# Products of keys with themselves taken two heads at a time, in the thirds that also turn keys into tokens

## What is computed

```
gc = cumsum(g)
decay[i,j] = exp(gc[i] - gc[j])            for i >= j, else 0
lower[i,j] = beta[i] * (k[i] . k[j]) * decay[i,j]   for i > j, else 0
t_mat      = inverse(I + lower)
u = t_mat @ (beta * v);  w = t_mat @ (beta * k * exp(gc))
```

## Time and profile before

| | |
|---|---|
| median of 3 runs | 354.02 us (353.72 to 354.14) |
| the profiled execution | 354.62 us, span 352.8 us |
| TensorE busy (PE) | 345.2 us, 98% of the span |
| VectorE (DVE) | 269.7 us, 76% |
| ScalarE (ACT) | 220.5 us, 62% |
| GpSimd (POOL) | 61.0 us, 17% |
| TensorE's granted clock, mean | 0.998 of 2.4 GHz |

### The profile page before, as it was taken

One profiled execution on the slowest core, in us unless ns is written; L12 is line 12 of the kernel. 1 busy time (PEld: TensorE's weight loads), 2 busy tenths in 40 slices (PEclk: granted clock), 3 DMA queues, 4 the chain that ended last, 5 costly groups with the idle time before them and its releaser, 6 DMA issues.

```text
span 352.8 us, 7457 instructions
## 1 busy us (share of the span) xinstructions
PE 345.2 (98%) x2753; PEld 332.2 (94%) x2753; DVE 269.7 (76%) x565; ACT 220.5 (62%) x499; POOL 61.0 (17%) x112
## 2 busy tenths in 40 slices
PE   8999999999999999999999999999999999999993
PEld 6889998999999999999999999999999999999882
DVE  4869897499986868978789797887967557588644
ACT  4778895455466667686866867677667655444421
POOL 2535535500033000300203011030200201000011
PEclk9999999999999999999999999999999999999999
DMA  7958948996799564655555565655555556775703
GB/s 233 274 140 225 304 125 201 236 289 171 209 248 218 134 180 126 163 133 153 146 150 149 131 170 129 171 132 146 143 159 143 171 158 181 208 240 186 260 32 119
DMA packets 100321, 62.48 MB, mean 177 GB/s; under 512 B 4692, under 2 KB 95230, under 8 KB 100286
## 3 DMA queue, kind: packets, MB, share of 16 engines
q1 hardware_dynamic: 98030, 58.59, 60.6%
q0 software_dynamic: 1072, 3.04, 3.0%
q10 hardware_dynamic: 1184, 0.39, 0.5%
HBM read 60.41 MB, written 1.59 MB: 176 GB/s over the span
## 4 chain that ended last, share of the span: by engine, by line
PE 97%; DVE 1%; issue 1%; POOL 0%; ACT 0%; DVEq 0%; POOLq 0%; ACTq 0%
PE banks L1347 67%; PE banks L1365 6%; PE banks L1560 6%; PE banks L1256 2%; PE banks L1445 1%; PE banks L1422 1%; PE banks L1462 1%; PE banks L1451 1%; PE banks L1332 1%; PE banks L1291 1%; PE banks L1507 1%; PE banks L1479 1%; PE banks L1483 1%; PE banks L1512 1%; PE banks L1487 1%
## 5 line engine op out<-in xcount | busy, mean ns | idle before, releaser
L890 DVE TENSOR_TENSOR w_lo<-raw,w_hi 128x1024 fp32r<-128x1024 f32 x102 | 124.1, 1218 | 44.4 <-ACT w_hi L637 43.9
L637 ACT CAST w_hi<-raw 128x1024 fp32r<-128x1024 f32 x103 | 107.5, 1047 | 10.0 <-PE banks L1560 5.5
L1347 PE MATMUL banks<-h_hi,w_hi 128*128 128x256 f32 x568 | 81.4, 286 | 0.0
L1347 PE MATMUL banks<-h_hi,w_lo 128*128 128x256 f32 x568 | 76.6, 278 | 0.0
L1347 PE MATMUL banks<-h_lo,w_hi 128*128 128x256 f32 x568 | 76.6, 278 | 0.0
L1347 PEld LDWEIGHTS banks<-h_hi,w_hi 128*128 128x128 f32 x568 | 71.0, 189 | 0.3
L1347 PEld LDWEIGHTS banks<-h_hi,w_lo 128*128 128x128 f32 x568 | 69.9, 188 | 0.0
L1347 PEld LDWEIGHTS banks<-h_lo,w_hi 128*128 128x128 f32 x568 | 69.9, 188 | 0.0
L974 DVE SCALAR_TENSOR_TENSOR acc<-banks,vec,acc 128x255 f32<-128x255 f32 (+2 forms) x72 | 34.5, 479 | 4.0 <-ACT acc L761 2.1
L587 POOL TENSOR_TENSOR so<-so,rnq 128x2 f32<-128x2 f32 x8 | 2.6, 328 | 162.8 <-ACT junk L828 162.8
L761 ACT ACTIVATE acc<-banks,vec 128x256 f32<-128x256 f32 x16 | 7.6, 474 | 18.7 <-PE banks L1347 18.7
(11 more groups left out here) (243 smaller groups left out, 548.3 us busy)
## 6 DMA issues: line engine op xcount, KB each, us to landing
raw<-in_w_in_dram SPq DMA_DIRECT2D x79, 512.0 KB, 4.0
raw<-in_w_branch_dram SPq DMA_DIRECT2D x16, 512.0 KB, 3.7
raw<-in_w_out_dram SPq DMA_DIRECT2D x8, 512.0 KB, 3.3
xin<-in_x_dram SPq DMA_DIRECT2D x2, 512.0 KB, 3.9
th_E<-g_rows POOLq DMA_DIRECT2D x2, 512.0 KB, 6.6
bias<-bias_rows POOLq DMA_DIRECT2D x1, 1024.0 KB, 8.2
raw<-in_x_dram SPq DMA_DIRECT2D x2, 512.0 KB, 4.4
out_dram<-xin SPq DMA_DIRECT2D x4, 256.0 KB, 2.0
```

The costliest lines, as they stand in the source:

```text
L637: nc.scalar.copy(w_hi[:, t % SLOTS, :], raw[:, t % SLOTS, :]).then_inc(s_hi, 1)
L890: v.tensor_tensor(w_lo[:, t % SLOTS, cols], raw[:, t % SLOTS, cols], w_hi[:, t % SLOTS, cols].bitcast(F32), ALU.subtract).then_inc(s_lo, 1)
L1347: last = mm(ps, w, r, start=part == 0 and k == 0, stop=part == 2 and k == KT - 1)
```

## The change

Three tables of step numbers change, and the two loops that read `SIM` now take a tuple of heads.

- The products of a head with itself are issued for two heads in one third: heads 0 and 1 at S = 27, 2 and 3 at S = 32, 4 and 5 at S = 36, 6 and 7 at S = 42. VectorE's multiplications for these heads stand at the same step numbers.
- The turns of heads 6 and 7 go from S = 35 and 41 to 36 and 42. With that each of the four thirds that holds products also holds a turn, and ScalarE's squares for these heads stand at S = 37 and 43.
- `E0` goes from 26 to 24, so ScalarE's exponentials for head h stand at S = 24 + h.

```diff
-TOKENS = {10: 0, 16: 1, 19: 2, 24: 3, 27: 4, 32: 5, 35: 6, 41: 7}
-SIM = {28: 0, 29: 1, 30: 2, 31: 3, 36: 4, 37: 5, 42: 6, 43: 7}
-E0 = 26
+TOKENS = {10: 0, 16: 1, 19: 2, 24: 3, 27: 4, 32: 5, 36: 6, 42: 7}
+SIM = {27: (0, 1), 32: (2, 3), 36: (4, 5), 42: (6, 7)}
+E0 = 24
...
-                if S in SIM:
-                    similarity(SIM[S])
+                for j in SIM.get(S, ()):
+                    similarity(j)
```

## The result

The changed kernel takes 355.58 us (median of 20 executions), the kernel before 354.11 us (20 executions, 353.72 to 354.59). The ratio is 1.0029, with an interval of 1.002 to 1.0038: slower by 0.3%. I had forecast no change, 353.9 us within 353.1 to 354.9.

A forecast was written before the change was run, and what follows sets the result against it. TensorE, with 97% of the chain, was taken to bound the kernel. From the profiled 354.62 us, minus 0.17 for breaks plus 0.1 for a wait gave 354.55, so a median of about 353.9 us, range 353.1 to 354.9.

The forecast's parts named there:

- what bounds: Whole kernel: TensorE holds 97% of the chain and shows no wait after start-up; faster ScalarE or VectorE is worth nothing.
- the work: TensorE: the change adds and removes no instruction, with 32 key product records and 16 turn records; term 0.
- the breaks: TensorE, S = 27 to 43: eight of twelve breaks go, saving 0.17 us, with bounds 0 and 0.9 us.
- the new wait: TensorE's turn of head 5 at S = 32 waits for its keys, 0 to 0.15 us; taken as 0.1.
- the price of a break beside key thirds: TensorE: a key third between breaks takes 0.95 us, 0.04 over the plain 0.907; three such breaks go.
- The rival with drains: TensorE: every break drains the array, so eight breaks would give back 1.3 us, 352.7 us; chance 4%.
- Term: 0: Blocks' store, load and inversion, 0.7 to 0.8 us later: margin at 113.68 shrinks from 1.2 to 0.5 us and holds.
- the inversion starts at 70.7: VectorE's inversion after the load of the blocks was to start at 70.7 us instead of 69.97.
- The slower rival: The blocks' store lands late, deciding from 5.2 us on; TensorE waits 1.4 us at S = 54, 355.3 us; chance 8%.

The follow-up runs named there:

- e12: Kernel before with the turns of heads 6 and 7 one third later (S = 36 and 42), run again for another trace: 355.17 us.
- e7: Kernel before with only the turns of heads 6 and 7 one third later (S = 36 and 42): 354.79 us, ratio 1.0022.
- e11: The changed kernel run once more, unmodified, for another trace: 354.00 us.
- e8: Changed kernel with the turn of head 7 back at S = 41 and the exponentials back at S = 26: 353.98 us, ratio 0.9995.
- e6: Kernel before with the turn of head 5 two thirds sooner, at S = 30, so TensorE must wait for its keys: 355.55 us.
- e5: Changed kernel with the turn of head 5 and products of heads 2 and 3 at S = 33 instead of 32: 355.05 us, ratio 1.002.
- e13: Kernel before with ScalarE's queue issuing the load of the blocks at S = 52 instead of 50: 354.22 us, ratio 1.0002.
- e16: The changed kernel run again, unmodified, for a third trace: 354.23 us.
- e15: Kernel before with the load of the blocks at S = 52 instead of 50, run again for another trace: 354.03 us.
- e18: The changed kernel run again, unmodified, the last of four repeats for more traces: 354.33 us.
- e17: The changed kernel run again, unmodified, the third of four repeats for more traces: 354.33 us.
- e4: Changed kernel with the products of head 7 one third later, at S = 43: 354.85 us, ratio 1.0028.
- e2: Changed kernel with the exponentials back at S = 26 to 33 (E0 = 26): 354.61 us, ratio 1.0018.
- e10: Changed kernel with step 9 of the inversion moved on VectorE from S = 68 to 69, behind the subtraction of tile 24: 354.68 us, ratio 1.0019.
- e9: Changed kernel with the turn of head 7 alone back at S = 41: 354.15 us, ratio 1.0004.
- e1: Changed kernel with TensorE turning head 7's keys once more at S = 51, results unused: 355.73 to 356.47 us, ratio 1.0063.
- e14: Kernel before with TensorE turning head 7's keys once more at S = 51, results unused: 354.47 us, ratio 1.0006.
- e3: Kernel before with the exponentials alone two thirds sooner (E0 = 24): 354.29 us, ratio 1.0009.

## Why the prediction was wrong

**Right: what bounds and the work; the breaks in their sum, partly by luck.** From the turn at S = 27 to the plain stretch at S = 48 the kernel before takes 64.37 - 40.51 = 23.86 us on TensorE's timeline (e12 and e7, with their twelve breaks, 23.82 and 23.92). The lowest trace of the changed kernel (e11) takes 63.73 - 40.00 = 23.73. That is 0.13 us saved, with what was left of the new wait in it, where I had 0.17; e8, with five breaks and no wait, takes 23.72. The lower group of the changed kernel, and e8 at ratio 0.9995, show that this is all that pairs are worth here. But what I read as the price of a break beside key thirds, 0.95 us against 0.907, was mostly something else: in those three thirds the products follow one another at 118 ns and not at 113, which is 8 x 4.4 ns = 0.035 us of the 0.04. In e11 the same three thirds run at 113 ns, without breaks between them:

```profile
41.28 2.75 PE banks L1347 x24
```

That is 0.09 us under 0.95 + 0.94 + 0.95 and most of the 0.13. The rival with drains (1.3 us) is out: the drain of 166 ns that the Trainium skill gives for a lone warm bf16 product (TensorE: Matmul & The Clock Gate, Single matmul latency) is no price for a break here, where 0.13 / 8 is 16 ns.

**Right: the new wait at S = 32, and its place.** I had the keys of head 5 at 46.1 to 46.35; they came at 45.57 + 0.42 = 45.99, and TensorE, which should have gone on at about 45.8, went on at 46.04: 0.24 us where I took 0.1. It costs its own length and no more, as e6 shows with a wait five times as long.

**Wrong: "Term: 0" for the blocks' way through memory.** This is the step that failed, in two places.

First, the size. I put the load's issue at 67.2 and it was 67.34. But I went on with "the inversion starts at 70.7", as if the load would take the 2.5 us of the kernel before. Issued 0.9 us later, it took up to 4.6 us in the changed kernel, 5.0 in e5, and 4.4 in e13, where nothing but its place was moved; in e8, issued at 65.91, it took 2.5. The time of issue alone doesn't set this: issued at 66.72 to 66.75 it took up to 2.7 us in e16, 4.0 in e15, 4.4 in e13 and 4.5 in e18. What it shares the queues with at that time I did not separate. So a delay of 0.9 us became one of 2.5. In the four traces of the lower group the load was issued from 66.05 to 67.08, and the inversion started at 70.27 to 71.82.

Second, the margin. I asked only whether the inverted blocks would be there at 113.68. That held for the time, though barely: VectorE waited for their load 0.3 us in e17 and 0.6 us in e18, at 113.8 and 114.1, TensorE in no trace. But the inversion is also *ahead of the weight subtractions* on VectorE. In the kernel before, the subtraction of tile 24 ended at 84.61 + 1.21 = 85.8, and TensorE needed it at S = 74, 26 thirds after 64.4, near 87.9: 2.1 us of margin, and I never took it from the trace. The margin of tile 28 is smaller still: its subtraction ended at 95.88 + 1.22 = 97.10, and TensorE needed it at S = 86, near 98.8, which leaves 1.7 us. VectorE's rows in the kernel before, tile 24 and then tiles 28 and 29:

```profile
84.61 1.21 DVE L890 TENSOR_TENSOR w_lo<-raw,w_hi 128x1024 fp32r<-128x1024 f32 x1
...
95.88 2.35 DVE L890 TENSOR_TENSOR w_lo<-raw,w_hi 128x1024 fp32r<-128x1024 f32 x2
```

The 2.5 us are above both, my 0.7 were not. So e12, e4 and e5 are held up at both tiles, e2 at tile 24, and e10, where tile 24 was helped, at tile 28. e17 and e13 (71.8 and 71.7) have 0.3 and 0.2 us left at tile 28, and e18 (71.8) nothing: it waits there for a quarter of a microsecond.

**The slower rival had the right place of origin and the wrong victim.** I had the store landing late, deciding from 5.2 us on and holding up the bank of tile 18, at 355.3, with 8%. The load was late without the store being that late (4.4 us at most in the trace of the changed kernel), and the bank was never waited for: the gate's tanh ran at 68.32 where I had 68.1. What waited was the subtraction, and the time was close (355.2 to 356).

**Not seen at all: the second pace.** Product after product at 118 ns instead of 113 is worth 1.69 us over the 48 plain thirds, more than everything in my sum. It was in the trace of before, in the chain of waits, where the same 24 products take 2.74 us in most places and 2.83 in some:

```profile
29.92 2.83 PE banks L1347 x24
```

I took no note of it, since I looked at what stands between thirds and not at the thirds. In that kernel the slow pace stands in stretches of one to three thirds between other pieces, from 28.6 to 44.4 us in every key third, and costs 0.035 us in each.

**What is shown and what isn't.** Shown: without the turn of head 7 at S = 42 the loss is gone, with everything else of the change in place (e9), and with the turns of heads 6 and 7 alone it is there (e7). Not shown is whether pairs or the wait at S = 32 make the upper group larger: it holds ten of nineteen executions of the changed kernel and four of twelve of e7. The loss is made before S = 96. It goes with an inversion from 72.26 on, through late subtractions, in e2, e4, e5, e10 and e12. Not settled: why TensorE takes the slow pace. Behind late subtractions it is there in all of those five traces, from 88 to 103 us on, in three of them only from the late taps at tile 30. In the changed kernel's first trace and in e1 it is there before anything late could reach TensorE, and I have no cause for it. A wait in this stretch doesn't do it (e6), nor does a small piece (e14), nor pairs, nor early exponentials (e8, e9, e3). Among kernels whose blocks are in time (e3, e6, e8, e9, e14 and before) no trace shows it in the plain thirds, and of 119 executions of the kernel before beside these runs one lay above 355.5 (356.70, at a mean clock of 0.987, where those below 355 had 0.995 to 0.999). Whether the upper group is mostly this or mostly waits stays open as well: the other four traces of the changed kernel all fell in the lower group. With eight of nineteen there, four in a row are one case in thirty, so the share need not be the same on every chip.

No version beat the kernel before clearly. The nearest is e8, pairs with the turn of head 7 and the exponentials where they were: 0.9995, with an interval that holds 1.

## What to carry to other kernels

When a step is moved by one place, follow it to the end of its chain and compare its delay with the margin of *everything* that is queued behind the last link, not only with the final consumer; here the inversion's own result was early enough, and the weight subtractions behind it were not. A small transfer through device memory had no fixed duration here, even when issued at the same time: price it at the spread of its neighbours, since a delay of 0.9 us turned into 2.5. And time a change in many executions before trusting a median or a single trace: six of the thirteen kernels timed here beside the kernel before had executions up to 2 us apart, and one profile shows one of them.

## What the hardware showed that I had not expected

- TensorE has two steady paces for the same products (128 by 128 weights, 256 columns, fp32r) at the same granted clock of 1.00: 113.4 ns and 117.8 ns. It keeps one over hundreds of products (384 in 43.54 or 45.23 us), with no wait in between, and changes it only where another piece or a late product stands between.
- Eight breaks between the weight stream and a few f32 products were worth 0.13 us in all, and most of that was the pace of three thirds beside them; none cost the 0.165 us by which a record outlasts its distance to the next.
- The same load of the blocks from device memory took 2.5 us when issued at 66.42, and when issued at 66.7 to 66.8 up to 2.7 us in one trace and up to 4.5 in another.
